# Linear-attention heads: level scores computed chunk by chunk in two column halves, and the products with scores and states placed behind the next round's first unit

## The chip, the cores and the metric

One core of one Trainium2 chip. The metric is the device time of one execution in microseconds. TensorE has two clock levels, 1.2 and 2.4 GHz; the profile shows the granted share of the higher one.

## The reference, cut to what matters

A model block of 512 tokens and width 1024 is followed by a second one. The change touches the second layer's mixer, a linear attention with gated decay, over 8 heads of 128 keys and 128 values, in chunks of 64 tokens:

```python
q, f_raw, i, g = jnp.split(h @ w_in, 4, axis=-1)
f = lb + (1.0 - lb) * jax.nn.sigmoid(f_raw)
log_f, k = jnp.log(f), 1.0 - f
bc = jnp.cumsum(to_chunks(log_f, HG_DK), axis=3)
def step(S, inp):                       # one chunk of 64 tokens, all heads
    qt, kt, vt, bt = inp
    decay = exp(where(tril, bt[:, :, :, None, :] - bt[:, :, None, :, :], -inf))
    scores = einsum('bhtk,bhsk,bhtsk->bhts', qt, kt, decay)
    o = scores @ vt + (qt * exp(bt)) @ S
    S = exp(b_last)[..., None] * S + (kt * exp(b_last - bt)).T @ vt
# then: o * rsqrt(mean(o*o) + EPS), times its gain and the gate g, and o @ w_out
```

## The kernel before

Activations lie with the 128 features of a block on the partitions and the 512 tokens on the free axis. Weights are streamed from HBM in units of 128 output columns by 1024 inputs (512 KB). Four slots `s` hold a unit each: SyncE loads it into `raw[s]`, ScalarE copies the high part to `w_hi[s]` (`act_hi`, L929), GpSimd subtracts it for the low part `w_lo[s]` (L361), and TensorE adds three products for each of 8 input blocks (`products`, L473 to L475, 24 matmuls of 512 columns a unit). Unit `s` ends in PSUM bank `s`.

The mixer handles one head a round, in `pe_hg`, `act_hg` and `dve_hg`, one function for each engine's queue. The order of work is the order in which these functions write it out; semaphores join the queues. Rounds 1 to 6 run in a hardware loop `Fori(0, 3)` with two heads in its body, round 0 stands ahead of it and round 7 behind.

In a round TensorE first computes the four units of the **following** head (forget gate, query, value, output gate, in that order, `units`), with the transposes of the former head's output behind the second (`turn_back`, L821). Then comes `mix`, the chunk work of this head: transposes of the decayed keys (L829, bank 4) and values (L834, bank 5); the scores; the products for the seven states (L854, banks 6 and 7); scores times values (L858, bank 5); and queries times states (L864), added to the same bank.

The decay inside a chunk can't be split into one factor per token without overflow, so scores are computed in seven levels. Level 0 is the diagonal: `hk` times `hq`. Levels 1 to 6 have `m` = 32, 16, 8, 4, 2, 1: blocks of 2m tokens, whose first half holds keys and whose second half holds queries, scaled by a decay relative to the middle (`hx[l-1]`, made by ScalarE's exponentials L1245 and VectorE's products L1809 from differences L1792). A level is four products of 128 by 128 tokens (L847), each over two chunks, into one of four banks. VectorE then takes from each level's bank the entries that the level's mask selects into `hs` (`copy_predicated`, L1845).

VectorE's and ScalarE's queues in a round: `decays` (cumulative sum L1779, differences, decayed keys `hkd` L1798, decayed queries `hqb` L1800, the levels' `hx`), `finish` (output times gain and gate into `hval`, L1827), `forget` of the following head (L1814, L1817, L1818), `low` (L1832, the low part of the finished head; `high` on ScalarE), `gate` (L1822), and the `mix` part: value copy (L1839), seven masked copies, seven states (L1852, L1855), and after ScalarE's root mean square (L1279, L933, L937) the normalisation (L1859). ScalarE's `take` reads the four unit banks and makes the next high parts. When the last head is done, four units of the output projection follow (`output`), of which the products with the first six heads stand ahead of round 7's chunk work for two units.

## Time and profile before

| | us |
|---|---|
| median of 3 runs | 2335.5 (2333.1 to 2338.34) |
| the profiled execution | 2337.77, its span 2336.1 |
| TensorE, matmuls busy in the span | 2211.3 (95%) |
| VectorE, ScalarE, GpSimd busy | 1056.3, 868.9, 915.0 |
| mean granted clock of TensorE | 0.980 |

TensorE's matmuls overlap each other in the records, so its work is best read from where one group starts to where the next does. The mixer's rounds lie between about 1622 and 1931 us of the span.

### The profile page before, as it was taken

How to read it: one execution, taken by the hardware profiler on the slowest of the kernel's cores; microseconds unless marked ns; L12 is line 12 of the kernel's file. 1: busy time of each engine (PE TensorE's matmuls, PEld its weight loads, DVE VectorE, ACT ScalarE, POOL GpSimd, SP SyncE). 2: the span in 40 equal slices, each digit the busy share in tenths (PEclk: the TensorE clock that was granted, in tenths of full speed). 3: DMA queues.
4: the chain of work that ended last, by engine and by line, in shares of the span. 5: the costliest groups of instructions: out<-in, count | busy, mean ns of one | idle time of the engine just before them, and what ended most of it. 6: DMA issues, size and time to landing. Idle time of an engine off the chain costs nothing.

```text
span 2336.1 us, 28554 instructions
## 1 busy us (share of the span) xinstructions
PE 2211.3 (95%) x10196; PEld 1785.3 (76%) x10196; DVE 1056.3 (45%) x1421; ACT 868.9 (37%) x1296; POOL 915.0 (39%) x445
## 2 busy tenths in 40 slices
PE   3899999989998999999999999998999989999997
PEld 1787767668886888887757888886888877888886
DVE  7413566664444222223965333203578766333201
ACT  5313534552323222334244332223555544233222
POOL 5322133234445444443714444443333214444442
PEclk8999999999998999999999999999999999999999
DMA  6312121116552222233213322232221112222232
GB/s 237 110 62 71 38 72 63 46 57 237 177 204 81 99 99 95 78 95 105 72 37 108 99 99 90 81 99 90 73 73 54 54 36 92 99 97 99 78 95 70
DMA packets 64701, 217.33 MB, mean 93 GB/s; under 512 B 7008, under 2 KB 8160, under 8 KB 64384
## 3 DMA queue, kind: packets, MB, share of 16 engines
q1 hardware_dynamic: 64640, 216.52, 28.2%
q8 instruction: 38, 0.62, 0.1%
q14 instruction: 23, 0.19, 0.0%
HBM read 214.40 MB, written 2.10 MB: 93 GB/s over the span
## 4 chain that ended last, share of the span: by engine, by line
PE 66%; DVE 8%; ACT 4%; issue 3%; DVEq 0%; ACTq 0%
PE ps L473 20%; PE ps L475 20%; PE ps L474 20%; DVE hs L1845 1%; DVE acc L1608 1%; PE ps L767 1%; DVE hx L1809 1%; PE ps L864 1%; ACT L937 1%; DVE h_lo L1571 1%; DVE hd L1792 1%; DVE r_lo L1832 1%; DVE hlf L1818 0%; ACT h_hi L1128 0%; PE ps L858 0%
## 5 line engine op out<-in xcount | busy, mean ns | idle before, releaser
L361 POOL TENSOR_TENSOR w_lo<-w_raw,w_hi 128x1024 fp32r<-128x1024 f32 (+2 forms) x376 | 860.5, 2297 | 1367.1 <-ACT w_hi L929 1366.8
L473 PE MATMUL ps<-h_hi,w_lo 128*128 128x512 f32 x1920 | 757.4, 394 | 17.8 <-DVE h_lo L1571 5.6
L475 PE MATMUL ps<-h_hi,w_hi 128*128 128x512 f32 x1920 | 750.8, 391 | 0.0
L474 PE MATMUL ps<-h_lo,w_hi 128*128 128x512 f32 x1920 | 750.8, 391 | 0.0
L929 ACT ACTIVATE w_hi<-w_raw 128x1024 fp32r<-128x1024 f32 (+2 forms) x376 | 370.9, 995 | 509.9 <-PE ps L475 507.1
L473 PEld LDWEIGHTS ps<-h_hi,w_lo 128*128 128x128 f32 x1920 | 363.3, 189 | 101.8 <-DVE h_lo L1571 6.9
L475 PEld LDWEIGHTS ps<-h_hi,w_hi 128*128 128x128 f32 x1920 | 362.6, 189 | 76.5
L474 PEld LDWEIGHTS ps<-h_lo,w_hi 128*128 128x128 f32 x1920 | 363.0, 189 | 75.4 <-issue 1.3
L473 PE MATMUL ps<-gu_hi,w_lo 128*128 128x512 f32 x528 | 205.4, 389 | 0.0
L474 PE MATMUL ps<-gu_lo,w_hi 128*128 128x512 f32 x528 | 205.4, 389 | 0.0
L475 PE MATMUL ps<-gu_hi,w_hi 128*128 128x512 f32 x528 | 205.4, 389 | 0.0
L1659 DVE TENSOR_TENSOR gu_lo<-fval,gu_hi 128x512 f32 (+1 forms) x66 | 129.5, 1963 | 65.0 <-ACT gu_hi L1180 65.0
L1583 DVE TENSOR_TENSOR x<-ps,x 128x512 f32<-128x512 f32 x32 | 21.9, 686 | 224.7 <-PE ps L475 224.7
L1653 DVE TENSOR_TENSOR fval<-ps,rstd 128x512 f32<-128x512 f32 x44 | 30.4, 692 | 201.3 <-PE ps L475 201.3
L473 PEld LDWEIGHTS ps<-gu_hi,w_lo 128*128 128x128 f32 x528 | 99.1, 188 | 20.7
L474 PEld LDWEIGHTS ps<-gu_lo,w_hi 128*128 128x128 f32 x528 | 99.1, 188 | 20.6
L475 PEld LDWEIGHTS ps<-gu_hi,w_hi 128*128 128x128 f32 x528 | 99.1, 188 | 20.4
L1176 ACT ACTIVATE sa<-sa 128x512 f32<-128x512 f32 x44 | 27.8, 632 | 164.6 <-DVE sa L1649 164.6
L1644 DVE TENSOR_TENSOR fval<-sa,ps 128x512 f32<-128x512 f32 x22 | 15.1, 687 | 147.0 <-PE ps L475 147.0
L1721 DVE SCALAR_TENSOR_TENSOR ps<-a_sb,vec,ps 128x512 f32<-128x512 f32 x87 | 62.1, 751 | 1.5
L1649 DVE TENSOR_TENSOR sa<-ps,rstd 128x512 f32<-128x512 f32 x44 | 30.4, 691 | 61.1 <-PE ps L475 50.1
L847 PE MATMUL ps<-hx 128*128 128x128 f32 x384 | 47.5, 286 | 6.6 <-DVE hs L1845 6.6
(330 smaller groups left out, 2523.1 us busy)
## 6 DMA issues: line engine op xcount, KB each, us to landing
w_raw<-in_w_ffn_in SPq DMA_DIRECT2D x132, 512.0 KB, 3.2
ada_w<-in_w_ada SPq DMA_DIRECT2D x48, 512.0 KB, 4.7
w_raw<-in_w_hg SPq DMA_DIRECT2D x40, 512.0 KB, 3.2
w_raw<-in_w_ffn_out SPq DMA_DIRECT2D x48, 384.0 KB, 3.1
w_raw<-in_w_conv_gate SPq DMA_DIRECT2D x32, 512.0 KB, 3.2
w_raw<-in_w_merge SPq DMA_DIRECT2D x32, 512.0 KB, 4.9
w_raw<-in_w_ffn_out SPq DMA_DIRECT2D x48, 320.0 KB, 2.9
w_raw<-in_w_cp SPq DMA_DIRECT2D x20, 512.0 KB, 3.4
```

What stands on the lines that cost most here:

```text
L361: pool.tensor_tensor(w_lo[s][:, 0:n], raw[s][:, 0:n], w_hi[s][:, 0:n].bitcast(F32), ALU.subtract).then_inc(lo_done[s], 1)
L473: pe.matmul(out, wl, hi, start=first, stop=False)
L474: pe.matmul(out, wh, lo, start=False, stop=False)
L475: return pe.matmul(out, wh, hi, start=False, stop=last)
L767: pe.matmul(ps[:, 4, :], tap[i % 4][:, :], a_sb[:, 2, i:i + T], start=(i == 0), stop=(i == CONVW - 1))\
L847: mm = pe.matmul(ps[:, l % banks, cols], a[:, cols], b[:, cols], start=True, stop=True)
L929: act.activation(w_hi[s][:, 0:n], raw[s][:, 0:n], ACT.Copy).then_inc(hi_done[s], 1)
L1176: act.activation(sa[p][:, :], sa[p][:, :], ACT.Silu).then_inc(S[f"ffn_sa{p}"], 1)
L1649: dve.tensor_tensor(sa[p][:, :], ps[:, 2 * p, :], rstd[:, :], ALU.mult).then_inc(S[f"ffn_scaled{p}"], 1)
L1653: dve.tensor_tensor(fval[p][:, :], ps[:, 2 * p + 1, :], rstd[:, :], ALU.mult)\
L1659: dve.tensor_tensor(at_index(gu_lo, 2 * r + p), fval[p][:, :], at_index(gu_hi, 2 * r + p).bitcast(F32), ALU.subtract).then_inc(S[f"ffn_lo{ ...
L1721: ins = dve.scalar_tensor_tensor(out=out, in0=src, scalar=w, in1=conv_ps[j], op0=ALU.mult, op1=ALU.add)
```

## The change

Four things change in the three functions of the mixer; sizes, weights, DMAs and all else stay.

- **Scores by chunk.** A level is eight products, one a chunk of 64 tokens: 64 stationary columns, the output in partitions 0 to 63 or 64 to 127 by the chunk's parity. In levels 1 to 6 the moving operand and the output are the second halves of the blocks alone, 32 columns. The masked copies of these levels take only those columns.
- **Order on TensorE.** `mix` is split. `within` holds the transposes, scores and states' products. `across` holds scores times values and queries times states, waits once for all seven states, and stands behind the following round's first unit; the turn back stands behind the third unit. `within` waits for the former head's low part ahead of its first transpose.
- **Order on ScalarE and VectorE.** The root mean square stands inside the next head's `decays`, ahead of level 3's exponentials, and the normalisation ahead of the work of the fifth level; `log` stands behind the key copy; the decayed queries and the states' decays stand at the end of `decays`; `forget` precedes `finish`; `high` stands behind the third unit's copy.
- **PSUM in place of two buffers.** The sigmoid of the forget gate and the gated output stay in their PSUM banks (0 and 4) in place of `hsf` and `hval`; bank 0 is free when `forget` has read it (`hf_ready`).
- **The end.** Three output units in place of two stand ahead of round 7's chunk work, which uses the three banks 6, 7 and 1 in place of 0 and 1; its states' products wait for all masked copies.

```diff
-            def mix(g, par, heads_taken, banks=4):
+            def within(g, par, heads_taken, banks):
                 pe.wait_ge(S["hkd_ready"], g + 1)
-                wait_former(pe, S["hval_ready"], g)
+                wait_former(pe, S["r_lo"], g)
...
-                    for c in range(TT):
-                        cols = slice(c * P, (c + 1) * P)
-                        a, b = (hk[par], hq[par]) if l == 0 else (hx[l - 1], hx[l - 1])
-                        mm = pe.matmul(ps[:, l % banks, cols], a[:, cols], b[:, cols], start=True, stop=True)
+                    bank = banks[l % len(banks)]
+                    for n in range(NCH):
+                        cols, rows = slice(n * CH, (n + 1) * CH), slice(n % 2 * CH, n % 2 * CH + CH)
+                        if l == 0:
+                            mm = pe.matmul(ps[rows, bank, cols], hk[par][:, cols], hq[par][:, cols], start=True, stop=True)
+                        else:
+                            mm = pe.matmul(later(ps[rows, bank, cols], l), hx[l - 1][:, cols],
+                                           later(hx[l - 1][:, cols], l), start=True, stop=True)
...
+            def across(g):
                 pe.wait_ge(S["hg_scores_read"], 7 * g + 7)
                 for c in range(TT):
                     pe.matmul(ps[:, 5, c * P:(c + 1) * P], hs[:, c, :], hv_tok[:, c, :], start=(c == 0), stop=False,
                               skip_group_check=True)
                 pe.wait_ge(S["hqb_ready"], g + 1)
+                pe.wait_ge(S["hg_state"], 7 * g + 7)
                 for n in range(1, NCH):
-                    pe.wait_ge(S["hg_state"], 7 * g + n)
...
-                          between=lambda: turn_back(2 * m + p))
-                    mix(2 * m + (1 + p), 1 - p, 2 * m + (3 + p))
+                          {0: lambda: across(2 * m + p), 2: lambda: turn_back(2 * m + p)})
+                    within(2 * m + (1 + p), 1 - p, 2 * m + (3 + p), (0, 1, 2, 3))
...
             with act.Fori(0, 3) as m:
                 for p in range(2):
-                    decays(2 * m + (1 + p), 1 - p)
+                    decays(2 * m + (1 + p), 1 - p, between=lambda: root(2 * m + p))
                     take(2 * m + (2 + p), p, between=lambda: high(2 * m + p))
-                    mix(2 * m + (1 + p))
+                    key_rows(2 * m + (1 + p))
+                    log(2 * m + (2 + p))
...
+                    m = LEVELS[l - 1]
+                    mask = level_mask[:, l - 1, :].bitcast(U32).rearrange("p (b a m) -> p b a m", a=2, m=m)[:, :, 1, :]
+                    dve.copy_predicated(hs[:, :, :].rearrange("p c (b a m) -> p c b a m", a=2, m=m)[:, :, :, 1, :],
+                                        mask.unsqueeze(1).broadcast_to([P, TT, P // (2 * m), m]),
+                                        bank.rearrange("p (c b a m) -> p c b a m", c=TT, a=2, m=m)[:, :, :, 1, :])
...
             with dve.Fori(0, 3) as m:
                 for p in range(2):
-                    decays(2 * m + (1 + p), 1 - p)
+                    decays(2 * m + (1 + p), 1 - p, between=lambda: normalise(2 * m + p))
+                    forget(2 * m + (2 + p), p)
                     finish(2 * m + p, p)
-                    forget(2 * m + (2 + p), p)
                     low(2 * m + p)
                     gate(2 * m + (2 + p), p)
-                    mix(2 * m + (1 + p), 1 - p)
+                    within(2 * m + (1 + p))
```

The end on TensorE, after the change:

```python
            begin(2)
            output(2, 0, 6)
            across(6)
            begin(3)
            output(3, 0, 6)
            begin(0)
            output(0, 0, 6)
            turn_back(6)
            within(7, 1, None, (6, 7, 1))
            for s in (2, 3, 0):
                output(s, 6, 7)
            across(7)
            pe.wait_ge(lo_done[1], Q_HGO + 1)
            output(1, 0, 7)
            turn_back(7)
            for s in range(4):
                output(s, 7, 8).then_inc(unit_done[s], 1)
```

## Rows read from the trace of the kernel before

**Rows 1.** The page: the chain that ended last, shares by engine

```profile
PE 66%; DVE 8%; ACT 4%; issue 3%; DVEq 0%; ACTq 0%
```

**Rows 2.** Windows: stretch, its length, busy time and records by engine, granted clock, DMA

```profile
1679.56:1886.82 207.26, 201.74 (x1202) 170.99 (x1201) 161.76 (x306) 111.54 (x234) 60.24 (x24) 1.00 0.19 61
1668.08:1679.56 11.48, 11.43 (x101) 10.20 (x99) 8.73 (x23) 2.03 (x3) 5.31 (x3) 1.00 0.53 175
```

**Rows 3.** Timeline of TensorE in a looped round: start, us, record count, idle before

```profile
1701.97 0.60 PE L829 MATMUL ps<-ident,hkd 128*128 128x128 f32 x4
...
1702.84 1.06 PE L847 MATMUL ps<-hq,hk 128*128 128x128 f32 x8
...
1709.18 1.16 PE L854 MATMUL ps<-hv_tok,hkd_tok 64*128 64x128 f32 x14
1711.29 1.16 PE L858 MATMUL ps<-hv_tok,hs 128*128 128x128 f32 x8 [0.95 <-DVE hs L1845]
1712.38 1.81 PE L864 MATMUL ps<-hst,hqb 128*64 128x128 f32 x14
1714.12 0.50 PE L473 MATMUL ps<-h_hi,w_lo 128*128 128x512 f32 x1
...
1725.14 0.60 PE L821 MATMUL ps<-ident,ho_tok 128*128 128x128 f32 x4
...
1736.51 0.60 PE L829 MATMUL ps<-ident,hkd 128*128 128x128 f32 x4
```

**Rows 4.** Windows of L864 alone: length, matmuls and weight loads started by its end (x)

```profile
1712.37:1712.40 0.03, 0.02 (x2) 0.02 (x2) 1.00 0.00 0
1712.37:1712.45 0.08, 0.07 (x2) 0.07 (x4) 1.00 0.01 0
...
1712.37:1712.80 0.43, 0.42 (x8) 0.42 (x8) 1.00 0.00 0
```

**Rows 5.** Timeline of VectorE in a looped round

```profile
1744.18 0.73 DVE L1845 COPY_PREDICATED hs<-level_mask,ps 128x512 f32<-128x512 uint32 x1
...
1745.04 0.72 DVE L1845 COPY_PREDICATED hs<-level_mask,ps 128x512 f32<-128x512 uint32 x1
...
1745.97 2.26 DVE L1855 SCALAR_TENSOR_TENSOR hst<-hst,hdec,ps 128x128 f32<-128x128 f32 x6
1753.58 0.69 DVE L1859 TENSOR_TENSOR ho_tok<-ps,o_rstd 128x512 f32<-128x512 f32 x1 [5.35 <-ACT o_rstd L937]
1754.19 1.21 DVE L1779 TENSOR_TENSOR_SCAN hb<-keep,hlf 128x512 f32<-128x512 f32 x1
...
1758.14 0.68 DVE L1792 TENSOR_TENSOR hd<-hb 128x512 f32<-128x512 f32 x1
1758.74 0.42 DVE L1809 TENSOR_TENSOR hx<-he,hk 128x256 f32<-128x256 f32 x1
...
1759.42 0.68 DVE L1792 TENSOR_TENSOR hd<-hb 128x512 f32<-128x512 f32 x1
...
1767.80 2.63 DVE L1818 TENSOR_SCALAR hlf<-hlf 128x512 f32<-128x512 f32 x1
```

**Rows 6.** Timeline of ScalarE in the same round

```profile
1748.76 0.28 ACT L1279 ACTIVATE hsquares<-ps 128x128 f32<-128x128 f32 x1 [10.02 <-PE ps L864]
...
1764.81 1.28 ACT L1253 ACT_TABLE_LOAD   x1
```

**Rows 7.** Timeline of the first round, all engines: its first masked copy

```profile
1670.12 0.75 DVE L1845 COPY_PREDICATED hs<-ident,ps 128x512 f32<-128x512 uint32 x1
```

**Rows 8.** Windows in the first block, columns as in rows 2

```profile
298.80:302.20 3.40, 1.46 (x10) 1.14 (x11) 2.71 (x6) 1.12 (x5) 2.35 (x1) 1.00 0.51 154
302.20:305.60 3.40, 3.40 (x10) 2.28 (x10) 1.28 (x3) 0.00 (x0) 0.00 (x0) 0.50 0.43 154
```

**Rows 9.** Timeline of TensorE at the mixer's end

```profile
1907.11 0.80 PE L847 MATMUL ps<-hx 128*128 128x128 f32 x2 [6.61 <-DVE hs L1845]
...
1930.49 0.39 PE L473 MATMUL ps<-r_hi,w_lo 128*128 128x512 f32 x1
```

More of the change, by code:

```diff
@@ L805, in pe_hg, with later, units @@
         def pe_hg(pe):
-            taken = ("hg_f_read", "hg_q_read", "hg_i_read", "hg_g_read")
-            def units(w, free, between=None):
+            taken = ("hf_ready", "hg_q_read", "hg_i_read", "hg_g_read")
+            def later(ap, l):
+                m = LEVELS[l - 1]
+                return ap.rearrange("p (b a m) -> p b a m", a=2, m=m)[:, :, 1, :]
+            def units(w, free, after={}):
                 for s in range(4):
@@ L812, in units @@
                     pe_unit(pe, s, s, w + Q_HG, h_hi, h_lo)
-                    if s == 1 and between:
-                        between()
+                    if s in after:
+                        after[s]()
             def turn_back(g):
@@ L851, in mix @@
                 wait_former(pe, S["hg_state"], 7 * g)
+                if 6 in banks:
+                    pe.wait_ge(S["hg_scores_read"], 7 * g + 7)
                 for n in range(7):
@@ L871, in pe_hg @@
             units(1, lambda s: pe.wait_ge(S[taken[s]], 1))
-            mix(0, 0, 2)
+            within(0, 0, 2, (0, 1, 2, 3))
             last_score = (5, 6, 7, 4)
@@ L1228, in log, with decays @@
                 act.activation(hlf[:, :], hlf[:, :], ACT.Ln).then_inc(S["hlog_ready"], 1)
-            def decays(g, par):
+            def decays(g, par, between=None):
                 act.wait_ge(S["hd_ready"], 7 * g + 1)
@@ L1234, in decays @@
                 act.activation(hkd[:, :], hd[0][:, :], ACT.Exp).then_inc(S["hd_used"], 1)
-                wait_former(act, S["ho_mm"], g)
-                act.activation(hqb[:, :], hb[par][:, :], ACT.Exp).then_inc(S["hqb_exp"], 1)
-                wait_former(act, S["hg_state"], 7 * g)
-                act.activation(hdec[:, :], hb[par][:, CH - 1:T:CH], ACT.Exp).then_inc(S["hdec_ready"], 1)
                 for i, m in enumerate(LEVELS):
+                    if i == 3 and between:
+                        between()
                     act.wait_ge(S["hd_ready"], 7 * g + i + 2)
@@ L1257, in take @@
                 act_hi(act, 1, q + 1)
-                if between:
-                    between()
                 act.wait_ge(unit_done[2], q + 1)
@@ L1262, in take @@
                 act_hi(act, 2, q + 1)
+                if between:
+                    between()
                 act.wait_ge(unit_done[3], q + 1)
@@ L1268, in high, with key_rows @@
                 wait_apart(act, S["hval_ready"], g + 1)
-                act.activation(at_index(r_hi, g), hval[:, :], ACT.Copy).then_inc(S["r_hi"], 1)
-            def mix(g, last=False):
+                act.activation(at_index(r_hi, g), ps[:, 4, :], ACT.Copy).then_inc(S["r_hi"], 1)
+            def key_rows(g):
                 act.wait_ge(S["hkd_mm"], g + 1)
@@ L1276, in mix, with root @@
                    .then_inc(S["hkd_tok_ready"], 1)
+            def root(g):
                 act.wait_ge(S["ho_mm"], g + 1)
@@ L1282, in mix @@
                 act.wait_ge(S["ho_ss"], 4 * g + 4)
-                act_power(act, o_rstd[:, :], o_ss[:, :], S["ho_rstd"], 2 * g, between=None if last else lambda: log(g + 1))
+                act_power(act, o_rstd[:, :], o_ss[:, :], S["ho_rstd"], 2 * g)
             take(0, 0)
@@ L1288, in act_hg @@
             take(1, 1)
-            mix(0)
+            key_rows(0)
+            log(1)
             with act.Fori(0, 3) as m:
                 for p in range(2):
-                    decays(2 * m + (1 + p), 1 - p)
+                    decays(2 * m + (1 + p), 1 - p, between=lambda: root(2 * m + p))
                     take(2 * m + (2 + p), p, between=lambda: high(2 * m + p))
-                    mix(2 * m + (1 + p))
-            decays(7, 1)
+                    key_rows(2 * m + (1 + p))
+                    log(2 * m + (2 + p))
+            decays(7, 1, between=lambda: root(6))
             high(6)
-            mix(7, last=True)
+            key_rows(7)
+            root(7)
             high(7)
@@ L1775, in dve_hg, with decays @@
         def dve_hg(dve):
-            def decays(g, par):
+            def decays(g, par, between=None):
                 k, qq, b = hk[par], hq[par], hb[par]
@@ L1875, in dve_hg @@
             gate(1, 1)
-            mix(0, 0)
+            within(0)
             with dve.Fori(0, 3) as m:
                 for p in range(2):
-                    decays(2 * m + (1 + p), 1 - p)
+                    decays(2 * m + (1 + p), 1 - p, between=lambda: normalise(2 * m + p))
+                    forget(2 * m + (2 + p), p)
                     finish(2 * m + p, p)
-                    forget(2 * m + (2 + p), p)
                     low(2 * m + p)
                     gate(2 * m + (2 + p), p)
-                    mix(2 * m + (1 + p), 1 - p)
+                    within(2 * m + (1 + p))
+            decays(7, 1, between=lambda: normalise(6))
             finish(6, 0)
-            decays(7, 1)
             low(6)
-            mix(7, 1, banks=2)
+            within(7, (6, 7, 1))
+            normalise(7)
             finish(7, 1)
```

60 lines of the change are left out of this document (31 added, 29 removed).

## The prediction, made before the changed kernel was run

> **What bounds the kernel now.** First the page's chain: two thirds of the span are TensorE's, and no other engine has a tenth [rows 1]. Then the stretch that the change touches, by the table of windows: the six looped rounds take 207.26 us, 34.54 each, and TensorE is busy for 201.74 of them; the first round's chunk work takes 11.48 [rows 2]. Then one round in TensorE's timeline [rows 3]. Two units take 11.02 us (1714.12 to 1725.14), and again 11.02 behind the turn back, which leaves 0.35 for the turn back. The chunk work is 12.15 us (1701.97 to 1714.12): transposes 0.87, scores 6.34 (1702.84 to 1709.18, 0.91 per level), states' products and a 0.95 us wait for the masked copies 2.11, products with scores 1.09, with states 1.74. So nearly everything that leaves TensorE's queue shortens the round, until the DVE/ACT loop that runs beside it (masked copies, states, decays, gate, copies again) closes last; the 0.95 us wait says that it is near. ScalarE and VectorE are followed in rows 5 and 6.
>
> **Score matmuls.** An fp32 product stands in the trace as two records. A level has now 8 records of 128 stationary and 128 moving columns, 0.91 us. After the change it has 8 products, so 16 records, of 64 stationary columns and 32 moving ones (64 at level 0), alternating between the two column halves. The trace has this form only with 128 moving columns, in L864. There the halves run side by side: two matmuls and two loads start within 0.03 us, and four loads have started within 0.08, so a second load follows the first of its half after about 0.055 us [rows 4]. With 32 moving columns the load should be the longer part. Eight slots of 0.055 make 0.44 us a level. The bounds: 0.054 us per matmul, the closest spacing that the trace shows (8 in 0.43, [rows 4]), makes 16 x 0.054 = 0.86; and halves that do not overlap make 16 x 0.112 = 1.79, 0.112 being 0.91/8. I take 0.44, being nearest to L864, and keep both others. Changing from whole-array to half-array matmuls costs about 0.1 us a time in these rows (L858 and L864 start late by that); the new order has one more change a round.
>
> The Trainium skill (TensorEngine Tiling, Key Properties) says that changing the tiling mode drains TensorE; the trace's 0.1 us agrees that it costs, and that it is small. The Trainium skill (TensorE: Matmul & The Clock Gate, "Wait — 56ns, not 53.3ns?") speaks against small matmuls: with hardware decoding off each MATMUL costs about 62 ns of issue. By that page a level would be an estimated 16 x 62 ns = 0.99 us, more than now. By it the rival below on issue would be true; no row of this trace decides it, since none has products short enough.
>
> **Masked copies.** Level 0 stays at 0.73 us, 0.87 with what precedes the next. The six others take every second block of columns, 256 in place of 512. DVE's products on 256 columns in the same patterns take 0.42 against 0.68 [rows 5], so I take 0.60 from copy to copy, in all 0.87 + 6 x 0.60 = 4.5 us against 6.1. Bound: 0.87 each, as now.
>
> **TensorE's round after.** Units 22.04, turn back 0.35; products with scores 1.09 and with states about 1.05 (7 slots of 0.11, two changes of form, no waits for single states, since all seven are awaited at once and are long done), now behind the next round's first unit: 24.6 us from the chunk work's end to the last unit's end. Then the chunk work. In the first round, which shows the undisturbed order, the first masked copy starts 2.04 us after the last unit (1668.08 to 1670.12, [rows 7]), behind sigmoid, gate and value copy. Four banks serve seven levels: levels 0 to 3 are done by then, level 4 waits for the read of level 0, 5 and 6 for those of 1 and 2. That puts level 6's end at 2.04 + 0.87 + 0.60 + 0.60 + 0.5 = 4.6, and the states' products (0.9, with two changes 1.2) at 5.8 to 5.9. Round: 24.6 + 5.9 = **30.5 us**, against 34.54.
>
> **The loop beside it.** From the first masked copy: copies 4.5, states 2.57 (0.31 for the first, 2.26 for the six others, [rows 5]), 7.05 to the scan. Then to the low part that TensorE now awaits before its transposes: scan, differences, decayed keys 3.35 (1754.19 to 1758.14 less the 0.6 of the decayed queries, which move back); three levels at 1.28. The root is now inside the levels: it starts on ACT 6.0 after the scan and takes 4.3 (1748.76 to 1753.58, less 0.5 for a logarithm; [rows 5, 6]), so 10.3; level 3 ends at 11.5, normalise 12.1, levels 4 and 5 14.1, decayed queries 14.85. ACT's table load 1.28 [rows 6] and sigmoid 16.0; forget in three PSUM steps 17.95, finish 18.6; ACT's six pieces up to the high part 20.4; low 21.1. To the next first copy another 1.8 (transposes, value copy). 7.05 + 21.1 + 1.8 = 30.0: 0.5 under TensorE's 30.5, and it hides. Two more table loads of 1.28 a round (five for three) fall in ACT's slack, ahead of its waits: the second logarithm's and the first exponential's lie while TensorE does the chunk work and VectorE the copies. If they did not hide, they would add 1.28 each. This path is shorter than now for one more reason: L1818, SBUF to SBUF, took 2.63 us while POOL made low weights [rows 5]; it and its two neighbours, and the subtraction for the low part, now read PSUM, which I price at 0.6 like the other steps on 512 columns (0.60 from 1758.14 to 1758.74). Nothing is moved past a wait of POOL or SP: POOL's first low part, 2.5 us, can start at 17 after the scan, some 20 us into the round, and is needed at 30.5; SP's loads follow POOL's as now. On ACT, the root now stands in front of the exponentials of levels 3 to 5, and VectorE's hx of level 3 waits for it: that is the 3 us gap counted above. On TensorE, the wait for the low part of the former head stands in front of all chunk work; its queue has nothing else to do then.
>
> The Trainium skill (VectorE: DVE Perf Modes, "Why PSUM operands drop a tier") says that an operand in PSUM leaves fp32 work at one element a cycle, without the two-port mode. By it the three forget steps cost more each than L1817's 0.43 now and nothing of the 2.63; the sum above has that already from rows.
>
> **Sum.** Loop 6 x (34.54 - 30.5) = 24.2. First chunk work 11.48 - 5.9 = 5.6. The end, counted from the loop's end: three output streams of 18 products at 0.23 (12.4), the products of round 6 (2.2) and the turn back bring TensorE to 15.9. Round 7's chunk work waits for the low part of round 6, behind all of VectorE's levels, at 3.4 + 14.85 + 2.1 = 20.4, so it idles 4.5 us; now it idles 6.61 in the same place [rows 9]. Transposes and value copy 21.9; copies 26.4, which the states' products must await (they reuse the banks) 27.5; six output products, last state 30; products with scores and states 32; root 4.3, normalise, turn back, finish, high, low 39.2. Now the last output products start at 43.7 (1930.49, [rows 9]). That is 4.5 us; if the clock halves behind that idle time, as it did where matmuls had been busy for 1.46 us of 3.40 [rows 8], the products that follow give about 3 back, so 1.4; I take 2.0. In all 31.8 us. The profiled execution took 2337.8 us (span 2336.1), so 2306.0; the median lies 2.3 lower: **2304**.
>
> **Rivals.**
> *Narrow matmuls bound by issue* (0.86 us a level): chunk work 6.0 + 2.15 = 8.15, round 32.75. 6 x 1.8 + 3.3 + 1.5 = 15.5 us, giving **2320**. For it: no row has matmuls closer than 0.054 on average. Against: pairs start within 0.03. Chance 0.15.
> *The clock falls in the chunk work.* It is 1.00 throughout the loop now. But after 3.40 us with matmuls busy for 1.46 it stood at 0.50 for 3.40 us [rows 8], and the new chunk work has transposes, half-empty products and short waits for 5.9 us. A fall each round costs 1.7 of matmuls, 7 x 1.7 = 12 us: **2316**. Against: the array is fed nearly all that time. Chance 0.12.
> *The DVE/ACT loop closes last* (copies stay at 0.87, or a table load shows): 30.0 + 1.6 = 31.6 a round, 7 us back: **2311**. Chance 0.13.
> *Slower: the halves run one after the other*, 1.79 a level: chunk work 14.7, round 39.3, +4.8 x 6 + 3.2, about **2369**. It turns to a loss from 1.1 us a level ((34.54 - 24.6 - 2.15)/7). L864 speaks against it. Chance 0.06.
> *Nothing gained*, about 1.1 us a level: 0.02.
> The forecast has 0.52, with a range of its own from 2297 (no idle, the end at 4.5) to 2310. The range that holds 8 in 10 adds the loop, clock and issue cases: **2297 to 2320**. A measurement tells about 0.2% (4.7 us) from no change. Faster 0.92, within 0.2% 0.02, slower 0.06.
>
> **What would show it.** Seven levels of score matmuls in about 3.2 to 4 us per round with starts some 0.03 apart; masked copies of about 0.47; a round of 30.5; TensorE without idle at L858 and L864; at most short idle ahead of the transposes, ended by the low part; the granted clock 1.00 in the loop. The forecast fails if 16 small records take more than 0.6 us a level, or if TensorE waits for the low part over 1 us a round.

## The result, and the profile after

| | before | after |
|---|---|---|
| median, us | 2336.35 (2333.1 to 2338.34, 4 runs) | 2308.62 (2307.1 to 2310.29, 4 runs) |
| the profiled execution | 2337.77, its span 2336.1 | 2308.86, its span 2307.1 |
| mean granted clock | 0.980 | 0.979 |

The ratio is 0.9874, with a 95% interval of 0.986 to 0.9888: 27.7 us less, where 2304 had been forecast from 2335.5, 31.5 less. The time lies in the range (2297 to 2320) and in the likeliest case's own (2297 to 2310).

Where it came from is read by stage, in the order of the prediction. The page's chain first, shares by engine: it answers to [rows 1], and TensorE is still the only engine with a tenth.

```profile
PE 69%; DVE 5%; ACT 3%; issue 2%; DMA 1%; DVEq 0%; ACTq 0%; SPq 0%
```

The windows of after, the same two stretches as in [rows 2], with the same columns: the six looped rounds, and the first round's chunk work.

```profile
1676.90:1858.95 182.05, 181.43 (x1537) 152.18 (x1536) 134.93 (x307) 125.82 (x246) 56.57 (x24) 1.00 0.21 69
1670.84:1676.90 6.06, 5.76 (x136) 5.29 (x134) 4.18 (x14) 5.23 (x6) 5.13 (x3) 1.00 0.70 237
```

The loop takes 182.05 us, 30.34 a round on average, 25.2 less in all than before (24.2 forecast). The first chunk work takes 6.06, 5.4 less (5.6 forecast). TensorE was busy for 201.74 of 207.26 before and is for 181.43 of 182.05 now, at a granted clock of 1.00: both the queue's own work and nearly all its waits became shorter.

The timeline of TensorE in a looped round of after, to set beside [rows 3]:

```profile
1731.92 0.63 PE L834 MATMUL ps<-ident,hkd 128*128 128x128 f32 x4
...
1732.91 0.69 PE L855 MATMUL ps<-hq,hk 128*64 128x64 f32 x16
1733.42 3.08 PE L857 MATMUL ps<-hx 128*64 128x32 f32 x96
1736.43 1.16 PE L867 MATMUL ps<-hv_tok,hkd_tok 64*128 64x128 f32 x14
1737.52 0.50 PE L473 MATMUL ps<-h_hi,w_lo 128*128 128x512 f32 x1
...
1743.13 1.05 PE L874 MATMUL ps<-hv_tok,hs 128*128 128x128 f32 x8
1744.11 1.09 PE L880 MATMUL ps<-hst,hqb 128*64 128x128 f32 x14
1745.13 0.50 PE L473 MATMUL ps<-h_hi,w_lo 128*128 128x512 f32 x1
...
1762.48 0.63 PE L834 MATMUL ps<-ident,hkd 128*128 128x128 f32 x4 [0.23 <-DVE r_lo L1859]
```

The scores, 6.34 us before, run from 1732.91 to 1736.43: 3.52, and 3.39 to 3.52 in all looped rounds. Scores times values and queries times states take 2.00 (1743.13 to 1745.13) behind the next round's first unit, and no idle time stands at them. What is left of waiting stands ahead of the transposes and is ended by the low part, as forecast. The window of L857 alone, from its first record on, answers to [rows 4]: 18 matmuls start in 0.47 us. After the first four records they start in pairs, one pair every 0.058 us, so 16 records take 0.44 from the first level's start to the second's, and 0.467 in the next three (0.44 forecast).

```profile
1733.42:1733.89 0.47, 0.47 (x18) 0.47 (x18) 1.00 0.65 150
```

The timeline of VectorE in the same rounds, which answers to [rows 5]: a forget step and the low part, both now reading PSUM, the value copy, and the masked copies of level 0, 1, 2 and 5.

```profile
1728.22 0.68 DVE L1845 TENSOR_SCALAR hlf<-ps 128x512 f32<-128x512 f32 x1
...
1731.08 0.69 DVE L1859 TENSOR_TENSOR r_lo<-ps,r_hi 128x512 f32 x1 [1.51 <-ACT r_hi L1288]
1732.58 0.69 DVE L1849 TENSOR_TENSOR hg<-hg,ps 128x512 f32<-128x512 f32 x1 [0.81 <-ACT hg L1283]
1733.18 0.68 DVE L1865 COPY hv_tok<-ps 128x512 f32<-128x512 f32 x1
1733.79 0.75 DVE L1872 COPY_PREDICATED hs<-ident,ps 128x512 f32<-128x512 uint32 x1
...
1735.26 0.45 DVE L1878 COPY_PREDICATED hs<-level_mask,ps 128x256 f32<-128x256 uint32 x1
1735.85 0.44 DVE L1878 COPY_PREDICATED hs<-level_mask,ps 128x256 f32<-128x256 uint32 x1
...
1737.85 0.74 DVE L1878 COPY_PREDICATED hs<-level_mask,ps 128x256 f32<-128x256 uint32 x1
```

The last forget step took 2.63 before [rows 5] and takes 0.68. The masked copies of levels 1 to 4 take 0.43 to 0.46, one about every 0.58 us (0.60 forecast); those of levels 5 and 6 take 0.74, one every 0.86. That was not in the forecast, and one experiment below is about it.

The end gained nothing. From the loop's end to the last head's output products 43.67 us passed before (1886.82 to 1930.49, [rows 2, 9]) and 44.04 pass now (1858.95 to 1902.99), where 2.0 less was forecast. What TensorE waits for there stands in the table of waits from 1676 to 1904 (who waits, for whom, us in all, times, longest):

```profile
PE ps L834 <- DVE r_lo L1859: 4.4, 3, 3.9
PE ps L473 <- DVE r_lo L1859: 2.2, 1, 2.2
PE ps L473 <- issue: 1.1, 1, 1.1
PE ps L867 <- DVE hs L1878: 0.9, 1, 0.9
```

Behind the loop these make 3.9 + 2.2 + 1.1 + 0.9 = 8.1 us. Before it was 6.6 [rows 9] and 1.5 ahead of the turn back of head 6 (the timeline of before, next), 8.1 too: TensorE waits elsewhere, not less.

```profile
1892.69 0.63 PE L821 MATMUL ps<-ident,ho_tok 128*128 128x128 f32 x4 [1.50 <-DVE ho_tok L1859]
```

The window around the end of the 3.9 us wait, and the timeline of TensorE in it:

```profile
1877.00:1893.00 16.00, 12.98 (x144) 11.81 (x145) 8.35 (x24) 1.19 (x2) 0.00 (x0) 0.57 0.01 2
```

```profile
1879.09 1.09 PE L834 MATMUL ps<-ident,hkd 128*128 128x128 f32 x4 [3.90 <-DVE r_lo L1859]
...
1881.87 5.28 PE L857 MATMUL ps<-hx 128*64 128x32 f32 x96
```

The granted clock stands at 0.50 from 1878.05 to 1891.7, 13.65 us (10.24 before), the lower of its two levels: six levels of scores take 5.28 there and 3.08 in the loop.

All later comparisons use one measure beside the whole time: **the mixer**, from the first key transposes to the last product of the output projection, in the profiled execution. It took 288.7 us before and takes 258.5 after, 30.2 less (31.8 forecast). A round, in what follows, runs from one head's key transposes to the next head's; ranges leave out the first looped round (30.87 in the changed kernel, whose others take 30.17 to 30.56; before, 34.35 to 34.74). The measure is needed because the whole time holds stretches that no edit here touches and that vary: the first key transposes stood at 1668.1 before, at 1670.8 after, and from 1664.1 to 1672.5 in the experiments.

### The profile page after: what moved, and what is told of

Same layout as the page of the kernel before. It is cut to its first block, busy times and chain, and to the rows that moved or that the text cites. A ratio compares the mean times of both kernels' runs of the same rounds, so it can differ in the third digit from the quotient of the medians.

```text
span 2307.1 us, 29442 instructions
## 1 busy us (share of the span) xinstructions
PE 2188.2 (95%) x10644; PEld 1763.1 (76%) x10644; DVE 1024.4 (44%) x1421; ACT 885.7 (38%) x1310; POOL 910.2 (39%) x445
## 4 chain that ended last, share of the span: by engine, by line
PE 69%; DVE 5%; ACT 3%; issue 2%; DMA 1%; DVEq 0%; ACTq 0%; SPq 0%
PE ps L473 22%; PE ps L474 21%; PE ps L475 21%; DVE acc L1633 1%; PE ps L767 1%; PE ps L857 1%; DVE h_lo L1596 1%; DMA x_res<-in_x 1%; ACT w_hi L947 0%; ACT h_hi L1146 0%; DVE hs L1878 0%; PE ps L709 0%; PE ps L624 0%; DVE x L1608 0%; PE ps L636 0%
## 5 line engine op out<-in xcount | busy, mean ns | idle before, releaser
L1583 DVE CUSTOM_DVE_ANT_0 ada_w<-ada_w,ps 128x1024 f32<-128x1024 f32 x32 | 38.3, 1215 | 32.1 <-DMA ada_w<-in_w_ada 32.1
```

The lines of the kernel that those rows point to most:

```text
L1583: dve.tensor_tensor_reduce(ada_w[i % 2][:, :], ada_w[i % 2][:, :], cond2, 1.0, 0.0, ALU.mult, ALU.add, accum_out=mod_sum[:, i:i + 1]).then ...
```

## The experiments

Each is the changed kernel with one edit, but where more edits or the kernel before are named. Ratios are to the kernel before, run on the same chip.

### Scores on the whole array again

```diff
-                    for n in range(NCH):
...
+                    for c in range(TT):
+                        cols = slice(c * P, (c + 1) * P)
+                        a, b = (hk[par], hq[par]) if l == 0 else (hx[l - 1], hx[l - 1])
+                        mm = pe.matmul(ps[:, bank, cols], a[:, cols], b[:, cols], start=True, stop=True)
```

> The changed kernel with only the score matmuls of before: a level is again four products of 128 by 128 tokens. If the score term is as I summed it, the chunk work grows from 5.6 us plus 0.4 of waiting to 0.97 + 6.35 + 1.2 = 8.5 us a round, the wait for the low part vanishes, and the time is 6 x 2.5 + 2.4 + some 3 at the lower clock in the last round = about 20 us above the changed kernel, 2328. If the new order alone made the gain and TensorE has slack, it is within 5 us of it.

Measured: 2325.77 us (2323.24 to 2329.35), ratio 0.9953 (0.9936 to 0.9969). The mixer takes 274.4, 15.9 more than after. Every looped round takes 32.87, and no wait is left in them. That is the 2.5 us a round that was expected; at the mixer's end less was lost than expected, with the granted clock at 0.50 for 6.8 us in the mixer in place of 13.65. The timeline of TensorE in one:

```profile
1733.31 1.06 PE L855 MATMUL ps<-hq,hk 128*128 128x128 f32 x8
...
1739.66 1.16 PE L864 MATMUL ps<-hv_tok,hkd_tok 64*128 64x128 f32 x14
```

The score phase (1733.31 to 1739.66) is 6.35 again, 2.9 more than the average of the changed kernel, but the round is only 2.5 longer: narrow scores also wait, for the low part and for banks that the masked copies must free.

### The two halves one after the other

```diff
-                    for n in range(NCH):
+                    for n in (0, 2, 4, 6, 1, 3, 5, 7):
```

> The changed kernel with each level's eight products in the order 0, 2, 4, 6, 1, 3, 5, 7, so that neighbours in the queue use the same column half. If the gain is the overlap of neighbours in different halves, a level costs up to 16 x 0.058 = 0.93 in place of 0.47 to 0.52, the score phase 6.3 in place of 3.4, a round 32.9, about 2326. If the halves overlap whatever the order, or narrow matmuls are simply cheaper, the time stays at 2308.

Measured: 2306.76 us (2306.51 to 2308.45), ratio 0.9867 (0.985 to 0.9883); rounds of 30.63 to 30.72, 0.3 longer than after; a score phase of 4.02. The 2326 us of halves that can't overlap did not come. The timeline of TensorE shows why: where one level ends, records of both kinds of score take turns (L855 is level 0, L857 level 1).

```profile
1730.84 0.79 PE L855 MATMUL ps<-hq,hk 128*64 128x64 f32 x13
1731.42 0.24 PE L857 MATMUL ps<-hx 128*64 128x32 f32 x1
1731.47 0.22 PE L855 MATMUL ps<-hq,hk 128*64 128x64 f32 x1
1731.49 0.22 PE L857 MATMUL ps<-hx 128*64 128x32 f32 x1
...
1734.86 1.16 PE L867 MATMUL ps<-hv_tok,hkd_tok 64*128 64x128 f32 x14
```

Level 1's first half of the columns runs beside level 0's second half. In this order 16 records take 0.52 us, against 0.467 when they alternate. So the products need not alternate one by one to overlap, and a version with the halves truly apart was not reached by this edit. The mixer takes 258.7, no more than in after, though its six looped rounds together are 1.7 us longer; the clock stood at 0.50 for 6.8 us in it, 13.65 in after.

### The old order with narrow scores and short copies

The kernel before, with the score matmuls and the masked copies of the change and nothing else of it.

> The kernel before with the first part of the change alone: scores by chunk and the masked copies of levels 1 to 6 over half the columns; order, buffers and the end stay as before. My theory: TensorE then waits for VectorE. Its loop in the old order is copies 4.9 in place of 6.1, and the rest of the loop 28.4 as before, so a round of about 33.4 in place of 34.54: 7 us for six rounds, 1.6 for the first and 2 for the last, about 10 below before, 2326 to 2328. Rival: TensorE's queue alone counts, then 3 us a round, 21 below before, 2315.

Measured: 2329.55 us (2324.23 to 2332.34, 8 runs), ratio 0.9962 (0.9951 to 0.9972). The mixer takes 280.1, 8.6 less than before, near the 10 that was expected. The four looped rounds at a granted clock of 1.00 take 32.40, 33.29, 33.51 and 33.05, near the 33.4 that was expected; the two others, at a mean of 0.90, take 34.59 and 34.45. The two longest waits in the table of TensorE's waits in its loop (the others make 1.9 us), and two windows of it:

```profile
PE ps L867 <- DVE hs L1861: 4.2, 4, 1.0
PE ps L855 <- DVE hs L1855: 3.6, 6, 0.6
```

```profile
1737.40:1740.80 3.40, 2.46 (x71) 2.18 (x68) 2.99 (x11) 0.16 (x1) 3.40 (x2) 1.00 0.43 158
1740.80:1747.60 6.80, 6.80 (x53) 5.96 (x52) 4.56 (x14) 0.01 (x1) 1.25 (x1) 0.50 0.44 157
```

The narrow scores are worth 15.9 us in the new order and, with the short copies, 8.6 in the old one. Part of what they free on TensorE turns into waits for VectorE, and twice in the loop the granted clock stood at 0.50 for 6.8 us, once behind the stretch shown. In the whole mixer it stood there for 27.3 us, 10.24 before, so the 8.6 us are what is left after this cost.

### The products with scores and states directly behind the chunk work

```diff
                     units(2 * m + (2 + p), lambda s: pe.wait_ge(S["hg_scores_read"], 14 * m + (7 * p + last_score[s])),
-                          {0: lambda: across(2 * m + p), 2: lambda: turn_back(2 * m + p)})
+                          {2: lambda: turn_back(2 * m + p)})
                     within(2 * m + (1 + p), 1 - p, 2 * m + (3 + p), (0, 1, 2, 3))
+                    across(2 * m + (1 + p))
```

> The changed kernel with the products with scores and states directly behind the states' products of the same head, as before, in place of behind the next round's first unit; all else stays. TensorE must then wait for the seven masked copies (6.9 us after the last unit) and the seven states (9.6): the round grows by about 3 us, 6 x 3 + 3 = some 20 us above the changed kernel, 2328. If the place of these products does not matter, because the loop beside TensorE closes last anyway, within 3 us.

Measured: 2333.39 us (2329.32 to 2339.05, 10 runs), ratio 0.9988 (0.9976 to 1.0): nearly all of the gain is gone. The mixer takes 282.9, 24.4 more than after. Its waits on TensorE from 1676 to 1920:

```profile
PE ps L880 <- DVE hst L1890: 9.4, 7, 1.4
PE ps L874 <- DVE hs L1879: 7.3, 7, 1.1
```

That is 2.4 us a round, and the round, 34.2 to 34.4, is 3.9 longer. The rest is seen in the windows of one round and in the timeline beside them:

```profile
1745.90:1749.30 3.40, 1.16 (x8) 0.98 (x9) 2.93 (x9) 0.00 (x0) 0.00 (x0) 1.00 0.28 108
1749.30:1752.70 3.40, 3.38 (x18) 2.78 (x19) 3.15 (x5) 1.24 (x3) 0.00 (x0) 0.50 0.00 0
```

```profile
1746.81 1.16 PE L874 MATMUL ps<-hv_tok,hs 128*128 128x128 f32 x8 [1.02 <-DVE hs L1879]
1749.32 1.94 PE L880 MATMUL ps<-hst,hqb 128*64 128x128 f32 x14 [1.35 <-DVE hst L1890]
```

With both waits in one stretch TensorE was busy for 1.16 of 3.40 us, and the clock then stood at 0.50 for 3.40: L880 takes 1.94 in place of 1.09. This came once behind each of the first seven heads' chunk work, 23.9 us; with 10.2 at the end the clock stood at 0.50 for 34.1 us of the mixer. It is what the prediction's clock rival feared: it doesn't arise in the changed kernel's loop, and it does as soon as the two waits are on TensorE's path.

This is not the order of before in full. `across` still waits for all seven states at once, where the kernel before waited for each state ahead of its own product and had no idle time at L864 [rows 3]. How much of the 24.4 us is that single wait (1.35 us of idle time a round, and its share in the fall of the clock), and how much the place of the products, no run here separates.

### All masked copies on 512 columns

```diff
-                    if l == 0:
-                        dve.copy_predicated(hs[:, :, :], ident[:, :].bitcast(U32).unsqueeze(1).broadcast_to([P, TT, P]),
...
+                    mask = ident[:, :] if l == 0 else level_mask[:, l - 1, :]
+                    dve.copy_predicated(hs[:, :, :], mask.bitcast(U32).unsqueeze(1).broadcast_to([P, TT, P]),
+                                        bank.rearrange("p (c t) -> p c t", t=P)).then_inc(S["hg_scores_read"], 1)
```

> The changed kernel with all masked copies over all 512 columns, as before. Levels 1 to 4 then cost 0.86 in place of 0.585 from copy to copy, 1.1 us more a round on the VectorE loop; that loop already closes last (TensorE waits 0.3 to 0.5 us a round for the low part), so the round grows by 1.1: 6 x 1.1 + 1 = about 7.5 us, 2316. If VectorE has slack, nothing. Levels 5 and 6, which measured 0.72 with half the columns, stay at 0.72 to 0.74.

Measured: 2318.17 us (2312.55 to 2320.12), ratio 0.9909 (0.9891 to 0.9927); rounds of 31.43 to 31.72, 1.3 longer than after (1.1 expected); the mixer 268.6, 10.1 more. The copies of levels 5 and 6 took the same 0.72 to 0.76 as all others. The waits of TensorE from 1676 to 1868, where those for the low part have grown:

```profile
PE ps L834 <- DVE r_lo L1859: 3.6, 5, 0.9
PE ps L857 <- DVE hs L1872: 1.5, 7, 0.2
```

### The two buffers in SBUF again

```diff
-                act.activation(ps[:, 0, :], ps[:, 0, :], ACT.Sigmoid).then_inc(S["hg_f_read"], 1)
+                act.activation(hsf[:, :], ps[:, 0, :], ACT.Sigmoid).then_inc(S["hg_f_read"], 1)
...
-                dve.tensor_scalar(hlf[:, :], ps[:, 0, :], 1e-19, None, ALU.max).then_inc(S["hf_ready"], 1)
+                dve.tensor_scalar(hlf[:, :], hlf[:, :], 1e-19, None, ALU.max).then_inc(S["hf_ready"], 1)
...
-                dve.tensor_tensor(at_index(r_lo, g), ps[:, 4, :], at_index(r_hi, g).bitcast(F32), ALU.subtract)\
+                dve.tensor_tensor(at_index(r_lo, g), hval[:, :], at_index(r_hi, g).bitcast(F32), ALU.subtract)\
```

> The changed kernel with the forget gate's sigmoid and the gated output again in SBUF buffers in place of their PSUM banks. If VectorE's last forget step and the low part's subtraction again wait for GpSimd's subtraction of 2.3 us, as L1818 (2.63) and L1832 (2.87) did, the loop beside TensorE grows by 2 to 4 us a round, less what is hidden: about 16 us above the changed kernel, 2325 (range 12 to 26 above). If that move is worth nothing because VectorE has slack, within 2 us.

Measured: 2318.07 us (2313.19 to 2318.44), ratio 0.9908 (0.9891 to 0.9924); rounds of 31.52 to 31.80, 1.3 longer; the mixer 266.4, 7.9 more. The timelines of VectorE and of GpSimd, and the waits of TensorE from 1676 to 1910:

```profile
1730.69 2.64 DVE L1846 TENSOR_SCALAR hlf<-hlf 128x512 f32<-128x512 f32 x1
...
1734.98 1.16 DVE L1860 TENSOR_TENSOR r_lo<-hval,r_hi 128x512 f32 x1 [0.98 <-ACT r_hi L1289]
```

```profile
1730.64 7.73 POOL L361 TENSOR_TENSOR w_lo<-w_raw,w_hi 128x1024 fp32r<-128x1024 f32 x3 [21.45 <-ACT w_hi L947]
```

```profile
PE ps L834 <- DVE r_lo L1860: 12.6, 7, 3.9
```

The 2.6 us step is back as soon as it reads SBUF, so it was the operands' place that shortened it. It makes the low part late, and the wait stands where the prediction says. SBUF alone does not make it slow: the trace puts its end about 0.3 us behind the end of the GpSimd subtraction that started 0.06 us ahead of it (1730.64 to 1733.05), and in this run's first round, where the step started 0.07 us ahead of GpSimd, it took 0.42. In the changed kernel the step from PSUM took 0.68 with a subtraction of 2.42 us running over it. The effect on the time was smaller than expected: the low part took 1.16 here, not the 2.87 of before, since it started when GpSimd's second subtraction had only 0.6 us to go (it ended at 1735.59).

### The high part earlier

```diff
-                act_hi(act, 2, q + 1)
                 if between:
                     between()
+                act_hi(act, 2, q + 1)
```

> The changed kernel with the high part of the finished head ahead of the third unit's weight copy on ScalarE (1.05 us earlier). If the wait ahead of the chunk work (0.3 to 0.5 us a round, ended by the low part) is ScalarE's chain, it vanishes: 6 x 0.4 = 2.4 us below the changed kernel, 2306. If something else ends it, no change.

Measured: 2306.64 us (2305.85 to 2308.28), ratio 0.9865 (0.9848 to 0.9881); rounds of 30.30 to 30.34; the mixer 258.5, exactly as after. The expectation of 2.4 us less failed, though the wait for the low part was gone. The timeline of TensorE:

```profile
1731.21 0.60 PE L834 MATMUL ps<-ident,hkd 128*128 128x128 f32 x4
...
1732.69 3.27 PE L857 MATMUL ps<-hx 128*64 128x32 f32 x96
...
1736.98 0.50 PE L473 MATMUL ps<-h_hi,w_lo 128*128 128x512 f32 x1
```

From the last unit's end to the next unit it is 5.77 us (1731.21 to 1736.98), and after's own is 5.77 too (1731.75 to 1737.52; 5.86 in two of its looped rounds), its wait included. The scores only took longer, 3.27 for six levels in place of 3.08, since they wait for banks. So the low part is not what sets the round: the first masked copy starts 2.04 us after the last unit's end in both (sigmoid, gate, value copy), and the copies set when the scores and the states' products can go.

### The value copy behind three masked copies

This has the edit of the experiment before too.

```diff
-                dve.tensor_copy(hv_tok[:, :, :].rearrange("p c k -> p (c k)"), ps[:, 5, :]).then_inc(S["hv_tok_ready"], 1)
                 for l in range(7):
+                    if l == 3:
+                        dve.tensor_copy(hv_tok[:, :, :].rearrange("p c k -> p (c k)"), ps[:, 5, :])\
+                           .then_inc(S["hv_tok_ready"], 1)
```

> The changed kernel with the high part ahead of the third weight copy, as in the run before, and the value copy on VectorE behind the third masked copy in place of ahead of the first. With the high part alone the wait ahead of the transposes went and the score phase grew by as much (3.73 for 3.41), the round staying at 30.3: the copies start 2.0 us after the last unit, whatever the low part does. If that is the bound, the copies now start 0.4 to 0.6 us earlier and the round falls to 29.9 to 30.0, TensorE's own sum: 2 to 2.5 us below the changed kernel. If VectorE's loop of levels closes last, the round stays at 30.3.

Measured: 2307.37 us (2300.18 to 2307.91), ratio 0.9857 (0.9836 to 0.9877); rounds of 29.99 to 30.20, 0.27 less than after on average; the mixer 255.9, 2.6 less. The first masked copy starts 1.70 us after the transposes (1732.87 to 1734.57), where it was 2.04 behind the last unit, and the round gains nearly the difference, which confirms the reading of the experiment before. The six rounds make 1.6 of the mixer's 2.6 us; the rest is at the end, where the clock stood at 0.50 for 10.24 us, 13.65 in after. The whole time can't tell it from the changed kernel.

### An earlier finish of the last but one head

`finish(6)` ahead of the last level's operands, `high(6)` and `low(6)` ahead of the decayed queries:

```diff
-            decays(7, 1, between=lambda: root(6))
-            high(6)
+            decays(7, 1, between=lambda: root(6), late=lambda: high(6))
...
-            decays(7, 1, between=lambda: normalise(6))
-            finish(6, 0)
-            low(6)
+            decays(7, 1, between=lambda: normalise(6), late=(lambda: finish(6, 0), lambda: low(6)))
```

> The changed kernel with a shorter way to the low part of round 6 at the mixer's end: its gated output stands ahead of level 6's hx on VectorE, its high and low parts ahead of the decayed queries. Round 7's chunk work can then start 1.6 us earlier and TensorE's idle time there falls from 4.1 to 2.5 us. If the granted clock then stays at 1.00 (it fell for 13.65 us), the end is 3 to 4 us shorter, 2305; if it falls all the same, 1 to 2 us, 2307.

Measured: 2306.37 us (2303.0 to 2306.81), ratio 0.9863 (0.9847 to 0.988). The last head's transposes start 24.24 us after the former head's, 25.73 in after: 1.5 earlier, as expected. But the mixer takes 257.8, only 0.7 less, and the clock stood at its lower level for 17.1 us in it, 13.65 in after. That the one took back the other's gain is not shown, as the next section tells.

### The three edits together, and the changed kernel once more

> The changed kernel with all three small edits: high part ahead of the third weight copy, value copy behind the third masked copy, and the shorter way to round 6's low part at the end. The rounds gave 30.1 in place of 30.36 with the first two (1.7 us) and the end 1.7 us with the third, so about 3 to 4 us below the changed kernel run beside it. If the effects don't add, 2.

> The changed kernel itself, unedited, beside the others on the same chip: 2308 to 2310, and rounds of 30.36. It is to show how much of the differences of 1 to 2 us between the small edits is no more than the run.

Measured on one chip: the three edits 2306.86 us (2302.26 to 2308.43), ratio 0.9867 (0.9845 to 0.9889), the mixer 255.6; the changed kernel 2304.96 (2303.32 to 2308.21), ratio 0.9868 (0.9849 to 0.9888), the mixer 258.3. The edits shorten the mixer by 2.7 us, 1.7 of it in the rounds, and no whole time that these runs can tell apart.

The repeat shows how far the clock at the end varies by itself. In the same kernel it stood at 0.50 for 10.24 us of the mixer, in three stretches, where the first execution had one of 13.65, and the mixer took 258.3 against 258.5. In the experiment below, whose rounds are the changed kernel's, it stood there for 3.41, and the mixer took 255.6. A difference of one to three microseconds in the mixer is therefore no proof of an edit's worth; the six looped rounds together, with the clock at 1.00, agree within 0.1 us in the three.

### The short masked copies with one operand packed

In the copies of levels 5 and 6, whose blocks are 2 columns and 1, one operand is read or written as 64 adjacent columns per block of 128 in place of every second short piece: the output in round 0, the mask in rounds 1, 3 and 5, the source in PSUM in rounds 2, 4 and 6, all three in round 7. The scores that these levels hand on are therefore not the reference's.

```diff
+                    if "m" in now:
+                        mask = mask[:, 0:H].rearrange("p (b m) -> p b m", m=m)
...
+                    if "o" in now:
+                        out = out[:, :, 0:H].rearrange("p c (b m) -> p c b m", m=m)
...
+                    if "s" in now:
+                        data = data[:, :, 0:H].rearrange("p c (b m) -> p c b m", m=m)
```

> What makes the masked copies of levels 5 and 6 (blocks of 2 and 1 columns) take 0.72 to 0.74 us on 256 elements, where levels 1 to 4 take 0.44. The changed kernel with one operand of these two copies taken from 64 adjacent columns in place of every second block: the output in round 0, the mask in rounds 1, 3 and 5, the PSUM source in rounds 2, 4 and 6, all three in round 7. The copies then move other entries, so attention outputs differ from the reference's; the time is read from each round's copies. If short pieces in the PSUM source cost, rounds 2, 4, 6 and 7 show 0.44 and the others 0.72; if it is the mask, rounds 1, 3, 5 and 7; if the output, rounds 0 and 7; if each piece of the whole pattern costs, only round 7.

Measured in one execution. The timeline of VectorE, a copy of level 6 in round 0 (output packed), of level 5 in rounds 2 (source) and 3 (mask), and of level 6 in round 7 (all three):

```profile
1671.61 0.45 DVE L1894 COPY_PREDICATED hs<-level_mask,ps 128x256 f32<-128x256 uint32 x1
...
1731.55 0.73 DVE L1894 COPY_PREDICATED hs<-level_mask,ps 128x256 f32<-128x256 uint32 x1
...
1761.98 0.72 DVE L1894 COPY_PREDICATED hs<-level_mask,ps 128x256 f32<-128x256 uint32 x1
...
1880.78 0.44 DVE L1894 COPY_PREDICATED hs<-level_mask,ps 128x256 f32<-128x256 uint32 x1
```

In nanoseconds, levels 5 and 6: output packed 441 and 449; mask packed 722 to 737; source packed 720 to 736; all packed 445 and 442. It is the output in pieces of one or two columns that costs 0.29 us a copy.

## Why the prediction was right

**What bounds it.** TensorE's queue, as read from [rows 1 to 3]: 25.2 us of the 30.2 came from the six looped rounds. The experiment with wide scores shows the link directly: 2.9 us more of scores, 2.5 us more of round.

**Score level.** 0.44 was forecast from [rows 4], 0.467 measured: the slot is 0.058, not 0.055. The issue rival (0.86) and the serial halves (1.79) are refuted in the changed kernel by 16 records in 0.467 us. The prediction's estimate of 0.99 from the Trainium skill (TensorE: Matmul & The Clock Gate, "Wait — 56ns, not 53.3ns?") did not come either: that section gives 62 ns a MATMUL for the case that hardware decoding is off, and here a record starts every 0.029 us on average.

**Masked copies.** The step that failed on size is "6 x 0.60". It held for four levels (0.58) and not for levels 5 and 6 (0.86 behind level 5), 4.9 us in all against 4.5 when every copy counts as a full step. The first state's copy follows the last masked copy after 0.54 already, so 4.60 passed from the first masked copy to the states. [Rows 5] had DVE's products into the same blocks, those of 2 and 1 columns too, and they take 0.42 for every level; only a row of the masked copy itself could have told.

**TensorE's round.** 30.34 against 30.5. From the chunk work's end to the last unit's end 24.6 (24.6 forecast), then 5.77 to 5.86 (5.9). The level 6 scores end 4.68 us after the last unit (4.6 forecast). The slow copies of levels 5 and 6 are not in this path, since the last level's products wait for the copy of level 2; they lengthen the loop beside it.

**The loop beside it.** The forecast let it close 0.5 us under TensorE. Its terms hold: 7.1 to 7.4 from the first copy to the scan (7.05 forecast), 21.2 from there to the low part's end (1741.15 to 1762.33; 21.1 forecast), 1.9 to the next first copy at 1764.21 (1.8). That these add up to the round is no finding, since they run from one first copy to the next. What shows that no slack is left is TensorE: in every looped round its transposes start 0.17 to 0.39 us behind the last unit, and with the high part earlier, this gap is gone; the forecast had the low part hidden. The table loads did hide, as forecast: behind those of logarithm and exponential ScalarE was idle for 6.02 us. The experiments tell what each path is worth. Without the low part's wait the round stays at 30.3; with the first copy 0.34 earlier besides, it is 30.1. With copies at 0.74 throughout, or with the steps in SBUF, this loop closes last and the round is 31.4 to 31.8, near the 31.6 of that rival.

**PSUM in place of SBUF.** The forecast took 0.6 a step, from start to start; the three forget steps start 0.85, 0.61 and 0.60 us apart and take 0.82, 0.69 and 0.68 each. The Trainium skill (VectorE: DVE Perf Modes, "Why PSUM operands drop a tier") says that such steps run without the faster mode; the trace agrees, with 0.68 where the same form in SBUF took 0.43 (it started ahead of GpSimd's subtraction), and shows the rest of the bargain, 2.64 gone.

**The end.** This step failed in its sign: 2.0 less was forecast, 0.4 more came. The transposes of round 7 start 20.1 us after the loop's end (20.4 forecast), behind 3.9 of idle time (4.5). That agreement is in part luck. The terms of TensorE's work ahead of it, 12.4, 2.2 and 0.35, make 15.0 and not the 15.9 of the forecast, and a wait of 1.1 us ahead of the first output unit was not in them. From there on the path falls behind, in us after the loop's end, forecast in brackets: first masked copy 23.2 (21.9), copies done 29.0 (26.4), states' products done 31.1 (27.5), last state 33.9 (30), products with scores and states done 36.0 (32), low part 44.0 (39.2). The loss is 4.8 us, where the forecast had set aside 2.5 for the clock. The clock accounts for about 3, an estimate from the same steps in the loop at 1.00: 1.2 from the transposes to the first copy (3.05 against 1.87), 1.0 in the copies (5.79 against 4.80, of which three banks in place of four may have a share) and 0.9 in the states' products (1.97 against 1.08). The rest is steps summed too short: 1.5 from the transposes to the first copy where the loop has 1.9, and 2.9 from the root to the low part where it was 3.6. What sets the length of the low stretches stays open: two executions of the same kernel had 13.65 and 10.24 us of them.

**The sum.** In it errors cancelled. The loop gave 1.0 us more than forecast, the end 2.4 less, the first chunk work 0.2 less, so 30.2 in place of 31.8. Of the 4.9 us between 2303.7, the forecast ahead of rounding, and 2308.6 the mixer has 1.6. The rest of the profiled execution has 1.2, and 2.1 come from the median, which was taken to lie 2.3 under the profiled execution, as before, and lay 0.2 under it.

**What each part was worth**, in the mixer, each taken out alone: the products with scores and states directly behind the chunk work, with the single wait for the states kept, 24.4 us (some of it clock), the narrow scores 15.9, the short copies 10.1, the PSUM buffers 7.9. They don't add up to 30.2: taking out any of them brings back waits between the same two paths. The scores and copies alone, in the old order, gave 8.6. Each of these numbers is from one profiled execution, and holds only to within the some 3 us by which the mixer's end varies.

## What to carry to other kernels

When work is taken off the engine that bounds a round, work out the loop of the other engines to the same precision, with each operand's pattern and memory, since the gain ends where that loop closes: here one part of the change alone gave 8.6 us, and with the order that kept the other engines' results off its path 30.2. Put consumers of a late result behind a long block of independent matmuls; here two waits of one microsecond in one stretch cost their own time and a halved clock behind it. When buffers are placed, look at which engine works on SBUF at the same time, and not at one operation's own duration alone. Judge an edit of a microsecond or two by a stretch of the profile that holds only what it touches.

## What the runs showed of the hardware

- Narrow fp32 score products (64 stationary columns, 32 moving) in alternating column halves start one record every 0.029 us on average, 16 in 0.467 us, against 8 whole-array records in 0.91. The halves also overlap when each half's four products stand together in the queue: 16 records in 0.52 us, and 4.02 us for seven levels against 3.39 to 3.52.
- A masked copy of 256 fp32 elements takes 0.43 to 0.46 us with output blocks of 32 to 4 columns, and 0.72 to 0.74 with blocks of 2 or 1. Packing the mask or the source in PSUM alone changed nothing (0.72 to 0.74); packing the output gave 0.44 to 0.45.
- An fp32 step of VectorE on 128x512 from SBUF to SBUF that started 0.06 us behind a GpSimd subtraction on SBUF took 2.64 us and ended 0.3 us behind it, in every looped round of the kernel before and of the run with SBUF buffers; 0.42 us where it started just ahead of one. From PSUM it took 0.68 with the subtraction running.
- A stretch of 3.40 us with matmuls busy for 1.16 was followed by 3.40 us at a granted clock of 0.50, and the same came once in each of the rounds of that experiment; in the changed kernel, where TensorE is busy for 181.43 of the loop's 182.05 us, it stayed at 1.00 throughout.
